# Serving a fifth of the tokens by fetched rows instead of dense expert tables, in a two-layer decoder step

## The chip, the cores and the metric

The kernel runs on one core of a Trainium2 chip. The metric is the device time of one execution in microseconds. TensorE multiplies matrices into the eight banks of PSUM, VectorE, ScalarE and GpSimd do the elementwise work between SBUF and PSUM, and DMA queues are fed by SyncE and GpSimd. Each engine runs its own instructions in order, and semaphores tie the engines together.

## What is computed

520 tokens (512 of a new sequence and 8 single ones) pass two layers. Layer 0 has a gated convolution beside attention, layer 1 a gated spatial mixer. After each comes an expert-retrieval mixer (PEER), which takes most of the time. For each token, and each of 8 heads, it picks 16 of 16,384 experts, an expert being one row of table U and one of table V, each 1024 floats:

```
q = (xf @ wq).reshape(n, PEER_HEADS, 2, PEER_DK // 2)
s = einsum('nhpd,hpkd->nhpk', q, keys);  top_s, top_i = top_k(s, 16)
best_s, pos = top_k(all 256 sums of a pair of top scores, 16);  gate = softmax(best_s)
hi = gelu(einsum('bed,bd->be', take(u_tab, ei), xi))      # 128 picks of each token
y  = einsum('be,bed->bd', gi * hi, take(v_tab, ei))
```

Then x becomes LayerNorm(alpha x + y). All is float32.

## The kernel before

Activations lie transposed: 8 blocks of 128 features in the partitions, 520 tokens in the columns. `xt` is x, `res` is alpha x, to which each mixer's result is added. A float32 product is made of three faster ones: ScalarE rounds a weight block to its high part (`whi`, `vhi`, `wth`), a subtraction gives the low part (`wlo`, `vlo`, `wtl`), and TensorE runs high x high, high x low and low x high.

The PEER mixer is dense: it computes every expert for every one of 512 tokens and masks with the gates. In each layer it has these stages.

**Queries.** `stage(C_WQ)` makes queries of 256 values per head for all 520 tokens, 16 chunks. GpSimd then loads the keys.

**First table.** 128 chunks (64 pairs, one slot of `whi`/`wlo`/`hid` each) of U, 128 experts a chunk: `chunk` runs 24 matmuls of 512 columns into `pstr[:, slot, 0]`, ScalarE takes gelu into `hid` (L753) and rounds the slot's next weights (L627), GpSimd makes the low part (L591), SyncE stores `hid` in HBM. Beside it runs the choice of experts, in five turns `w` of 104 tokens. TensorE computes the scores, VectorE ranks them (`topk`, some 160 short instructions in 48 parts, a Python generator), TensorE turns the picks, and ScalarE copies them to `pickt` (L800). In the next turn VectorE makes one-hot matrices of 4 tokens at a time (`one_hots`, L1311 once and L1314 four times), whose products on TensorE (L1553) are the dense gates; ScalarE copies them to `gst`, and SyncE stores them. `PLAN` gives the order: for each turn, how many pairs run with no gate group, with one behind each chunk, with two behind each chunk; ranking parts are dealt between one-hot groups by `RANK_PARTS` and `RANK_IN`.

**Second table.** 32 periods of 8 turns. A period covers 4 x 128 experts, a turn is 12 matmuls of 512 columns for one block of 128 output features (`second_table`, L1617). VectorE makes gated hidden values (`gated`, L1155 and L1157), their low part (L1162) and the low part of V (L1144), and adds each finished bank to `res` (`take_v`, L1170). ScalarE makes the two high parts (L821, L814). In a turn of even number the order on VectorE is gated, low part of V two turns ahead, add; on ScalarE it is high part of the gated values, then of V. The partial sums use two banks in turn.

The eight single tokens are not in the dense columns. GpSimd fetches their picked rows by indirect DMA (L604, 128 rows each, 8 times U and 8 times V a layer). VectorE multiplies and sums the rows of U (`sample_dot`, L1115) against x spread over all partitions by TensorE (L1637), and TensorE weights the rows of V (L1649).

Of the kernel before, what the change touches and what calls it, by code (L numbers as in the profile page):

```python
# [22 lines left out]
F32 = mybir.dt.float32  # L23
F32R = mybir.dt.float32r
# [29 lines left out]
WHOLE = SEQ // GH  # L54
# [13 lines left out]
assert all(2 * one + 4 * two == GROUPS for _, one, two in PLAN[1:])  # L68
# [16 lines left out]
DOTS_G, VALS_G = 1, 3  # L85
# [4 lines left out]
LN_OF = {2: 0, 3: 1, 5: 3}  # L90

# [32 lines left out]
def first_group(tt):  # L124

    return tt // NT * L_GROUPS + tt % NT * GROUPS

# [10 lines left out]
def trunk(nc, i, o):  # L138
    with ExitStack() as ctx:  # L139
# [17 lines left out]
        xl = place("xl", [P, KB, N], F32R)  # L157
        res = place("res", [P, KB, N], F32)
# [63 lines left out]
        s_id = place("s_id", [P, DEC], U32, choice_end + 2 * 4 * SEQ)  # L222
        s_idf = place("s_idf", [P, DEC], F32, choice_end + 2 * 4 * SEQ + 32)
        s_gate = place("s_gate", [P, DEC], F32, choice_end + 2 * 4 * SEQ + 64)

# [4 lines left out]
        wth = place("wth", [P, 2, GROUP, SEQ], F32R)  # L230
        wtl = place("wtl", [P, 2, GROUP, SEQ], F32R)
        gc = place("gc", [P, 2, 2 * NT, GROUP * GH], F32)
        hl = place("hl", [P, GROUP, SEQ], F32)
        wt = place("wt", [P, 2, SEQ], F32)


        rows = place("rows", [P, RING, D_MODEL], F32, at_xt)
        xr = place("xr", [DEC, 2, D_MODEL], F32R)
        pickr = place("pickr", [DEC, DEC], F32R)
        s_dots = place("s_dots", [P, DEC], F32)  # L240
        s_hid = place("s_hid", [P, DEC], F32)
        s_w = place("s_w", [P, DEC], F32)
        assert used[0] <= choice_end, used[0]

        hid = place("hid", [P, 2, SEQ], F32, choice_end)
        used[0] = choice_end + 2 * 4 * SEQ + 96
# [10 lines left out]
        gates = [nc.dram_tensor(f"gates{n}", (2 * NT, P, P, GH), F32, kind="Internal").ap() for n in range(DEPTH)]  # L257

        hidden = [nc.dram_tensor(f"hidden{n}", (P, P, SEQ), F32, kind="Internal").ap() for n in range(DEPTH)]
# [87 lines left out]

        s_listed = sem("s_listed")
        s_turned = sem("s_turned")
        s_rows = sem("s_rows")  # L350
        rows_in = [sem(f"rows_in{n}") for n in range(RING)]
        s_spread = sem("s_spread")
        s_dot = sem("s_dot")
# [1455 lines left out]
```

## Time and profile before

| | us |
|---|---|
| three runs | 4199.63, 4208.36, 4205.72; median 4205.72 |
| the profiled execution | 4195.6, its span 4193.8 |
| TensorE busy | 4040.5, 96% of the span |
| VectorE busy | 2710.7, 65% |
| ScalarE busy | 1478.5, 35% |
| GpSimd busy | 814.5, 19% |
| DMA | 648 MB, 155 GB/s on average |

Busy time is the union of an engine's instructions in the profiled execution. An engine that waits is not busy. TensorE's matmuls overlap, so the time one takes from start to end is longer than the distance from one start to the next, and it is the distance that adds up. The same holds by a smaller part for VectorE and ScalarE. Each layer's PEER mixer is some 1620 us: the first table from 572 and the second from 1452 us in layer 0, from 2555 and 3435 in layer 1.

### The profile page before, as it was taken

To read this page: it belongs to the slowest core of one execution; us is meant where nothing else is said; L and a number is where in the kernel's file an instruction comes from. 1 tells how busy PE (TensorE), PEld (TensorE's weight loads), DVE (VectorE), ACT (ScalarE), POOL (GpSimd) and SP (SyncE) were. 2 spreads that over 40 slices of the span, in tenths; PEclk is the share of its full clock that TensorE was granted. 3 is DMA by queue.
4 is the path that set the end of the run, shared out by engine and by line. 5 is a ranking of instruction groups with operands and counts; after the bars stand their busy time and mean duration, and the time that the engine had idled before them with its cause. 6 is when DMAs were issued, how large, how long until landed. Compare 5 with 4: busy or idle time off the path is not lost. (4 is left out here: it accounts for less than half of the span.)

```text
span 4193.8 us, 61594 instructions
## 1 busy us (share of the span) xinstructions
PE 4040.5 (96%) x20468; PEld 3334.9 (80%) x20468; DVE 2710.7 (65%) x5770; ACT 1478.5 (35%) x2092; POOL 814.5 (19%) x462
## 2 busy tenths in 40 slices
PE   8889899999999999999999899999999999999998
PEld 8734888888788788888879788888878878888887
DVE  2342367898887366777763336889889736677775
ACT  3221333444444322333334233444444432333333
POOL 4011123343333310000001012333333331000000
PEclk9989999999999999999999699999999999999999
DMA  4444233544454665655542023354444466555663
GB/s 121 126 141 137 77 111 121 172 154 150 148 172 146 237 216 171 201 193 195 189 138 71 25 76 115 117 177 153 146 165 152 167 215 219 189 191 186 199 198 106
DMA packets 315592, 648.24 MB, mean 155 GB/s; under 512 B 29496, under 2 KB 111544, under 8 KB 314832
## 3 DMA queue, kind: packets, MB, share of 16 engines
q1 hardware_dynamic: 302400, 606.66, 44.1%
q0 software_dynamic: 13072, 40.16, 3.2%
q8 instruction: 54, 0.88, 0.1%
q14 instruction: 66, 0.54, 0.0%
HBM read 507.09 MB, written 139.61 MB: 154 GB/s over the span
## 5 line engine op out<-in xcount | busy, mean ns | idle before, releaser
L591 POOL TENSOR_TENSOR wlo<-wraw,whi 128x1024 fp32r<-128x1024 f32 x252 | 646.9, 2568 | 1260.1 <-ACT whi L627 1260.1
L1356 PE MATMUL pstr<-xh,whi 128*128 128x512 f32 x2048 | 832.7, 407 | 12.0 <-POOL wlo L591 11.9
L1356 PE MATMUL pstr<-xh,wlo 128*128 128x512 f32 x2048 | 814.9, 398 | 0.0
L1617 PE MATMUL aux<-wth,vhi 128*128 128x512 f32 x2048 | 805.0, 393 | 7.1 <-DVE res L1170 7.1
L1356 PE MATMUL pstr<-xl,whi 128*128 128x512 f32 x2048 | 809.8, 395 | 0.0
L1617 PE MATMUL aux<-wth,vlo 128*128 128x512 f32 x2048 | 799.1, 390 | 0.0
L1617 PE MATMUL aux<-wtl,vhi 128*128 128x512 f32 x2048 | 798.7, 390 | 0.0
L1314 DVE TENSOR_SCALAR oh<-cst,pickt 128x128 f32<-128x128 f32 x1040 | 665.9, 700 | 0.0
L1144 DVE TENSOR_TENSOR vlo<-vraw,vhi 128x512 fp32r<-128x512 f32 x512 | 352.3, 688 | 325.7 <-ACT vhi L814 325.7
L821 ACT ACTIVATE wth<-wt 128x512 fp32r<-128x512 f32 x256 | 161.6, 632 | 933.7 <-DVE wt L1157 933.7
L753 ACT ACTIVATE hid<-pstr 128x512 f32<-128x512 f32 x256 | 152.8, 597 | 946.0 <-PE pstr L1356 931.8
L1356 PEld LDWEIGHTS pstr<-xh,whi 128*128 128x128 f32 x2048 | 388.7, 190 | 95.0 <-issue 15.1
L1356 PEld LDWEIGHTS pstr<-xh,wlo 128*128 128x128 f32 x2048 | 387.8, 189 | 92.1
L1617 PEld LDWEIGHTS aux<-wth,vhi 128*128 128x128 f32 x2048 | 385.6, 188 | 93.3 <-DVE vlo L1144 8.4
L1356 PEld LDWEIGHTS pstr<-xl,whi 128*128 128x128 f32 x2048 | 388.9, 190 | 84.6
L1617 PEld LDWEIGHTS aux<-wth,vlo 128*128 128x128 f32 x2048 | 385.3, 188 | 80.4
L1617 PEld LDWEIGHTS aux<-wtl,vhi 128*128 128x128 f32 x2048 | 385.7, 188 | 78.6
L1170 DVE TENSOR_TENSOR res<-res,aux 128x512 f32<-128x512 f32 x512 | 350.1, 684 | 135.1 <-PE aux L1617 133.3
L627 ACT ACTIVATE whi<-wraw 128x1024 fp32r<-128x1024 f32 x344 | 361.5, 1051 | 88.6 <-PE pstr L1360 85.9
L1311 DVE TENSOR_TENSOR oh<-cst,pickt 128x512 f32<-128x512 f32 x260 | 205.2, 789 | 227.5 <-PE aux L1553 169.5
L814 ACT ACTIVATE vhi<-vraw 128x512 fp32r<-128x512 f32 x512 | 298.7, 619 | 73.3 <-DMA vraw<-in_v 50.1
L889 DVE TENSOR_TENSOR wlo<-wraw,whi 128x1024 fp32r<-128x1024 f32 x92 | 113.3, 1233 | 325.4 <-ACT whi L627 325.4
(222 smaller groups left out, 4796.3 us busy)
## 6 DMA issues: line engine op xcount, KB each, us to landing
wraw<-in_u SPq DMA_DIRECT2D x256, 512.0 KB, 3.6
vraw<-in_v SPq DMA_DIRECT2D x512, 256.0 KB, 3.9
gates<-gst SPq DMA_DIRECT2D x80, 832.0 KB, 7.1
gc<-gates SPq DMA_DIRECT2D x64, 1040.0 KB, 5.5
hidden<-hid SPq DMA_DIRECT2D x256, 256.0 KB, 2.1
hl<-hidden SPq DMA_DIRECT2D x256, 256.0 KB, 4.9
wraw<-in_w SPq DMA_DIRECT2D x88, 512.0 KB, 3.5
kv<-in_ck SPq DMA_DIRECT2D x32, 256.0 KB, 3.2
```

The costliest lines, as they stand in the source:

```text
L591: e.tensor_tensor(wlo[:, slot, :], wraw[:, slot, :], whi[:, slot, :].bitcast(F32), ALU.subtract).then_inc(u_lo, 1)
L627: e.activation(whi[:, slot, :], wraw[:, slot, :], ACT.Copy).then_inc(w_hi, 1)
L753: e.activation(hid[:, slot, :], pstr[:, slot, 0, :], ACT.Gelu_apprx_tanh).then_inc(chunk_taken, 1)
L814: e.activation(vhi[:, v % 4, :], vraw[:, v % 4, :], ACT.Copy).then_inc(v_hi, 1)
L821: e.activation(wth[:, par, j, :], wt[:, j % 2, :], ACT.Copy).then_inc(wt_hi, 1)
L889: e.tensor_tensor(wlo[:, slot, :], wraw[:, slot, :], whi[:, slot, :].bitcast(F32), ALU.subtract).then_inc(w_lo, 1)
L1144: e.tensor_tensor(vlo[:, v % 4, :], vraw[:, v % 4, :], vhi[:, v % 4, :].bitcast(F32), ALU.subtract).then_inc(v_lo, 1)
L1170: e.tensor_tensor(r, r, aux[:, v % 2, :], ALU.add).then_inc(v_taken, 1)
L1311: e.tensor_tensor(oh2[:, slot], spread(c(IOTA), 1, shape), spread(pickt[:, 1, at:at + SUB], 2, shape), ALU.is_equal).then_inc(oh_ready, 1)
L1314: e.tensor_scalar(oh1[:, slot, r, :], c(IOTA), pickt[:, 0, at + r:at + r + 1], pickt[:, 2, at + r:at + r + 1], ALU.is_equal, ALU.mult).the ...
L1356: mm = e.matmul(pstr[:, slot, 0, :], w[:, slot, k * P:(k + 1) * P], x[:, k, 0:SEQ], start=k == 0 and w is whi and x is xh, stop=k == KB - ...
L1617: mm = e.matmul(aux[:, v % 2, :], w[:, v % 4, j * P:(j + 1) * P], x[:, par, j, :], start=j == 0 and w is vhi and x is wth, stop=j == GROUP ...
```

## The change

Of the 520 tokens the last 104 (`SPARSE`: one turn of the choice, which has the 8 single tokens and 96 others in it) leave the dense tables. `D` = 416 tokens stay, so every matmul, gelu, store and load of both tables has 416 columns. `hidden` and `gates` shrink accordingly, and gate groups fall from 130 to 104 a layer. The sparse tokens are ranked in the second turn (`ORDER`). Tokens lie in the partitions for them: one gather brings the row that pick j chose, for 104 tokens. A dot on VectorE against x (turned by TensorE in the query stage into two banks, `aux[:, 0:2]`) gives column j of `s_dots`. In the second table an add on VectorE sums 128 weighted rows of V into `acc`, which TensorE turns back at the end. GpSimd's loop is unrolled, with the gathers of U placed behind the low parts of given pairs.

The rows of U use the room of `res`, which is stored in HBM before (`keep`) and loaded again near the end. The second table's eight output blocks each stay in a bank of PSUM of their own over all 32 periods, so that `take_v` runs only in the last one. The one-hots read iota from a copy in PSUM. Scores go one round behind each of the first four chunks of a turn rather than all ahead of them.

```
+ND = 4
+D = ND * TT
+SPARSE = ND
+ORDER = [0, SPARSE, 1, 2, 3]
+NH = D // GH
-PLAN = [(6, 0, 0), (0, 11, 1), (0, 11, 1), (0, 9, 2), (0, 9, 2), (0, 1, 6)]
+PLAN = [(7, 0, 0), (2, 1, 6), (10, 0, 0), (2, 9, 2), (2, 9, 2), (0, 1, 6)]
-L_GROUPS = N // SUB
-EXP_AT = 17
+L_GROUPS = D // SUB
+EXP_AT = 20
-RANK_IN = 22
+RANK_FROM, RANK_TO = 1, 22
+DOTS = [0, 0, 22, 30, 30, 30]
+TAIL_DOTS = [10, 6]
+ADD_FROM, ADD_TO = 12, 236
...
+def share(n, total, begin, end):
+    return total * min(max(n - begin, 0), end - begin) // (end - begin)
+
+def row_pairs():
+    at, start = [], 0
+    for (zero, one, two), dots in zip(PLAN, DOTS):
+        for n in range(GROUPS):
+            if one + two:
+                pair = zero + (n // 2 if n < 2 * one else one + (n - 2 * one) // 4)
+                new = share(n + 1, dots, 0, GROUPS) - share(n, dots, 0, GROUPS)
+            else:
+                pair = 2 + n * (zero - 2) / GROUPS
+                new = share(n + 1, dots, 3, GROUPS) - share(n, dots, 3, GROUPS)
+            at += [start + pair] * new
+        start += zero + one + two
+    n = sum(TAIL_DOTS)
+    at += [start + TAIL * (k + 0.5) / n for k in range(n)]
+    return [int(at[max(j - RING, 0)]) + 1 for j in range(HJ)]
...
+        rows_u = place("rows_u", [P, RING, D_MODEL], F32, at_res)
+        rows_v = place("rows_v", [P, RING, D_MODEL], F32, at_xt)
...
+        v_banks = [aux[:, 2, :], aux[:, 3, :], pstr[:, 0, 1, :], pstr[:, 1, 1, :],
+                   pstr[:, 0, 0, :], pstr[:, 1, 0, :], aux[:, 0, :], aux[:, 1, :]]
+        iota = aux[:, 3, 0:P]
...
+                e.wait_ge(res_ready, 8 * (2, 4)[layer])
+                e.dma_start(keep[layer], res[:].rearrange("p k n -> p (k n)")).then_inc(res_out, 16)
                 load_u(0)
...
+                e.wait_ge(s_dot, (layer + 1) * HJ)
+                e.dma_start(res[:].rearrange("p k n -> p (k n)"), keep[layer]).then_inc(res_in, 16)
                 period(NG - 3, 1, True)
...
# GpSimd
+                def fetch_u(j):
+                    if j == 0:
+                        e.wait_ge(s_listed, layer + 1)
+                        e.wait_ge(res_out, 16 * (layer + 1))
+                    if j >= RING:
+                        e.wait_ge(s_dot, layer * HJ + j - RING + 1)
+                    e.indirect_dma_start(rows_u[0:TT, j % RING, :], None, i["ur"],
+                                         bass.IndirectOffsetOnAxis(ap=s_id[0:TT, j:j + 1], axis=0)).then_inc(rows_u_in[j % RING], 16)
-                with e.Fori(1, P // 2) as p:
+                fetch_at = row_pairs()
+                for p in range(1, P // 2):
                     for slot in range(2):
                         pair = p + C_U[layer] // 2
                         e.wait_ge(w_hi, pair * 2 + (slot + 1))
                         e.tensor_tensor(wlo[:, slot, :], wraw[:, slot, :], whi[:, slot, :].bitcast(F32),
                                         ALU.subtract).then_inc(u_lo, 1)
+                    for j in range(HJ):
+                        if fetch_at[j] == p or (fetch_at[j] > p and p == P // 2 - 1):
+                            fetch_u(j)
+                e.wait_ge(pick_ready, (layer + 1) * NT)
+                for j in range(HJ):
+                    if j >= RING:
+                        e.wait_ge(s_acc, layer * HJ + j - RING + 1)
+                    e.indirect_dma_start(rows_v[0:TT, j % RING, :], None, i["vr"],
+                                         bass.IndirectOffsetOnAxis(ap=s_id[0:TT, j:j + 1], axis=0)).then_inc(rows_v_in[j % RING], 16)
...
# VectorE
+                def sparse_dots(n):
+                    for _ in range(n):
+                        j = next(dots)
+                        if j == 0:
+                            e.wait_ge(s_turned, layer + 1)
+                            e.wait_ge(s_listed, layer + 1)
+                        e.wait_ge(rows_u_in[j % RING], 16 * (layer * (HJ // RING) + j // RING + 1))
+                        row = rows_u[0:TT, j % RING, :]
+                        e.scalar_tensor_tensor(row, row, 1.0, aux[0:TT, 0:2, :].rearrange("p a n -> p (a n)"), ALU.mult, ALU.mult,
+                                               accum_out=s_dots[0:TT, j:j + 1]).then_inc(s_dot, 1)
+                def sparse_add(j):
+                    e.wait_ge(rows_v_in[j % RING], 16 * (layer * (HJ // RING) + j // RING + 1))
+                    row, weight = rows_v[0:TT, j % RING, :], s_w[0:TT, j:j + 1]
...
+                        e.wait_ge(s_acc, layer * HJ + j)
+                        e.scalar_tensor_tensor(acc[0:TT], row, weight, acc[0:TT], ALU.mult, ALU.add).then_inc(s_acc, 1)
...
+                        for n in range(GROUPS):
+                            one_hots(layer * L_GROUPS + d * GROUPS + n, n % 2, n * SUB)
+                            for _ in range(share(n, RANK_PARTS, RANK_FROM, RANK_TO), share(n + 1, RANK_PARTS, RANK_FROM, RANK_TO)):
+                                next(ranking, None)
+                            sparse_dots(share(n + 1, DOTS[w], 0, GROUPS) - share(n, DOTS[w], 0, GROUPS))
...
+                for g in range(NG):
+                    par, more = g % 2, g + 1 < NG
+                    if not more:
+                        e.wait_ge(res_in, 16 * (layer + 1))
+                    for v in range(8):
+                        if more and v % 2 == 0:
+                            gated(g + 1, v // 2, 1 - par, (g + 1) // 2)
+                        elif more:
+                            split_wt(g + 1, v // 2, 1 - par)
+                        if v < 6:
+                            split_v(g, v + 2)
+                        elif more:
+                            split_v(g + 1, v - 6)
+                        if (g, v) == (1, 2):
+                            sparse_weights()
+                        while added < share(g * 8 + v + 1, HJ, ADD_FROM, ADD_TO):
+                            sparse_add(added)
+                            added += 1
+                        if not more:
+                            take_v(v)
+                        if not more and v in (4, 5):
+                            take_back(v - 4)
...
# one_hots
-                e.tensor_tensor(oh2[:, slot], spread(c(IOTA), 1, shape), spread(pickt[:, 1, at:at + SUB], 2, shape),
+                e.tensor_tensor(oh2[:, slot], spread(iota, 1, shape), spread(pickt[:, 1, at:at + SUB], 2, shape),
                                 ALU.is_equal).then_inc(oh_ready, 1)
                 for r in range(SUB):
-                    e.tensor_scalar(oh1[:, slot, r, :], c(IOTA), pickt[:, 0, at + r:at + r + 1],
+                    e.tensor_scalar(oh1[:, slot, r, :], iota, pickt[:, 0, at + r:at + r + 1],
                                     pickt[:, 2, at + r:at + r + 1], ALU.is_equal, ALU.mult).then_inc(oh_ready, 1)
...
# TensorE
+                def turn_x():
+                    e.wait_ge(ln_out, 8 * LN_OF[split] + 8)
+                    for k in range(KB):
+                        mm = e.transpose(aux[0:TT, k // 4, k % 4 * P:(k % 4 + 1) * P], xt[:, k, D:N], c(IDENT))
+                    mm.then_inc(s_turned, 1)
+                stage(C_WQ[layer], N_WQ, split, between=turn_x)
...
+                            mm = e.matmul(v_banks[v][:, 0:D], w[:, v % 4, j * P:(j + 1) * P], x[:, par, j, :],
+                                          start=isinstance(g, int) and g == 0 and j == 0 and w is vhi and x is wth,
+                                          stop=isinstance(g, int) and g == NG - 1 and j == GROUP - 1 and w is vlo)
```

## Rows read from the trace of the kernel before

**Rows 1.** Busy time of each engine by stage, granted clock, DMA share and GB/s last.

```profile
572.00:1452.00 880.00, 859.56 (x4286) 718.37 (x4285) 695.44 (x1708) 373.01 (x431) 328.37 (x130) 0.99 0.47 158
1452.00:2189.00 737.00, 733.05 (x3281) 604.18 (x3280) 499.07 (x902) 221.10 (x385) 14.43 (x14) 1.00 0.58 188
2555.00:3435.00 880.00, 859.70 (x4286) 718.60 (x4285) 695.29 (x1708) 372.99 (x431) 327.49 (x130) 0.99 0.47 158
...
1620.00:2100.00 480.00, 480.00 (x2119) 397.63 (x2119) 339.09 (x618) 151.54 (x264) 0.00 (x0) 1.00 0.60 193
```

**Rows 2.** Timeline: two chunks apart on ScalarE; matmuls of 260 columns. Start, duration.

```profile
1397.36 0.60 ACT L753 ACTIVATE hid<-pstr 128x512 f32<-128x512 f32 x1 [3.71 <-PE pstr L1356]
...
1408.52 0.60 ACT L753 ACTIVATE hid<-pstr 128x512 f32<-128x512 f32 x1 [4.12 <-PE pstr L1356]
...
540.10 0.40 PE L1360 MATMUL pstr<-xh,wlo 128*128 128x260 f32 x2
540.34 0.41 PE L1360 MATMUL pstr<-xh,whi 128*128 128x260 f32 x2
```

**Rows 3.** Timeline of TensorE, first matmuls of two chunks with a gate group between.

```profile
2720.87 0.48 PE L1356 MATMUL pstr<-xh,whi 128*128 128x512 f32 x1
...
2727.34 0.48 PE L1356 MATMUL pstr<-xh,whi 128*128 128x512 f32 x1
```

**Rows 4.** Timeline of VectorE, a ranking's first and last instructions.

```profile
576.11 3.19 DVE L1216 MAX8 tv<-scores 104x8 f32<-104x128 f32 x16 [2.39 <-ACT scores L780]
...
632.01 0.29 DVE L1301 TENSOR_TENSOR pick<-bv,gs 104x128 f32<-104x128 f32 x1
```

**Rows 5.** Groups of VectorE by shape: busy, mean ns of one, idle before.

```profile
L1115 DVE SCALAR_TENSOR_TENSOR rows<-rows,pstr 128x1024 f32<-128x1024 f32 x16 | 19.5, 1220 | 0.7
...
L1000 DVE SCALAR_TENSOR_TENSOR t<-zp,vec,t 128x512 f32<-128x512 f32 x8 | 6.0, 752 | 0.3
```

**Rows 6.** VectorE: one-hots in the timeline; MAX8's min/median/max; the one-hots' group.

```profile
3275.49 0.68 DVE L1311 TENSOR_TENSOR oh<-cst,pickt 128x512 f32<-128x512 f32 x1
...
3277.11 0.68 DVE L1311 TENSOR_TENSOR oh<-cst,pickt 128x512 f32<-128x512 f32 x1
...
3280.27 3.21 DVE L1314 TENSOR_SCALAR oh<-cst,pickt 128x128 f32<-128x128 f32 x4
...
L1216 DVE MAX8 tv<-scores x160: 264/275/296, 576.1 to 3129.2; 104x8 f32<-104x128 f32 x160
...
L1314 DVE TENSOR_SCALAR oh<-cst,pickt 128x128 f32<-128x128 f32 x1040 | 665.9, 700 | 0.0
```

**Rows 7.** Timeline of GpSimd, one split late in the first table.

```profile
1404.48 2.41 POOL L591 TENSOR_TENSOR wlo<-wraw,whi 128x1024 fp32r<-128x1024 f32 x1 [3.10 <-ACT whi L627]
```

**Rows 8.** The gathers: issue on GpSimd in ns, min/median/max; time to landing.

```profile
L604 POOL DMA_INDIRECT rows<-in_ur,s_id x16: 937/1146/1251, 1442.1 to 3489.7; - x16
...
DMA to landing us min/median/max: 4.1/4.9/7.7
```

**Rows 9.** The chain that ended last: start, us, one spread and one value round.

```profile
3466.63 1.12 PE pstr L1637 x4
...
3526.48 1.68 PE aux L1649 x16
```

**Rows 10.** Timelines of VectorE and ScalarE in the second table; then waits: us, times, longest.

```profile
3702.38 0.64 DVE L1155 TENSOR_TENSOR wt<-hl,gc 128x468 f32<-128x468 f32 x1
3702.93 0.20 DVE L1157 TENSOR_TENSOR wt<-hl,gc 128x44 f32<-128x44 f32 x1
3704.34 0.69 DVE L1144 TENSOR_TENSOR vlo<-vraw,vhi 128x512 fp32r<-128x512 f32 x1 [1.22 <-ACT vhi L814]
3704.95 0.68 DVE L1170 TENSOR_TENSOR res<-res,aux 128x512 f32<-128x512 f32 x1
...
3703.16 0.63 ACT L821 ACTIVATE wth<-wt 128x512 fp32r<-128x512 f32 x1 [3.77 <-DVE wt L1157]
...
ACT vhi L814 <- DMA vraw<-in_v: 50.1, 84, 1.4
```

More of the change, by code:

```diff
@@ L776, in peer @@
                     tt = w + layer * NT
-                    if w < NT:
+                    first = pair
+                    if w == 0:
                         for b in range(4):
-                            e.wait_ge(sc_done, tt * 4 + b + 1)
-                            e.activation(scores[0:TT, 4 * b:4 * b + 4, :].rearrange("p a k -> p (a k)"),
-                                         aux[0:TT, 2 + b % 2, :], ACT.Copy).then_inc(sc_taken, 1)
-                    if zero:
-                        hidden_pair(pair)
-                        with e.Fori(pair + 1, pair + zero - 2) as p:
+                            take_scores(tt, b)
+                    elif w < NT:
+                        for r in range(4):
+                            hidden_one(first + r // 2, r % 2)
+                            take_scores(tt, r)
+                        first += 2
+                    if zero and not one + two:
+                        if first == 0:
+                            hidden_pair(first)
+                            first += 1
+                        with e.Fori(first, pair + zero - 1) as p:
                             hidden_pair(p)
                         gate_exponentials(tt)
-                        for p in range(pair + zero - 2, pair + zero):
-                            hidden_pair(p)
+                        hidden_pair(pair + zero - 1)
                     n = 0
@@ L1363, in chunk, with stage @@
                 mm.then_inc(chunk_done, 1)
-            def stage(first, count, split, means=None):
+            def stage(first, count, split, means=None, between=None):
                 chunk(first, 0, 0, split)
                 chunk(first, 0, 1)
+                if between:
+                    between()
                 start = count // 2 - 3
@@ L1559, in first_table, with score_round @@
                         chunk(C_U[layer], pair, slot)
+                def score_round(w, b):
+                    tt, d = w + layer * NT, ORDER[w]
+                    if w and b == 0 and ORDER[w - 1] != SPARSE:
+                        e.wait_ge(pick_taken, layer * ND + ORDER[w - 1] + 1)
+                    if tt or b:
+                        e.wait_ge(sc_taken, tt * 4 + b)
+                    for q in range(4 * b, 4 * b + 4):
+                        mm = e.matmul(aux[0:TT, 2, q % 4 * P:(q % 4 + 1) * P], q_t[:, q, d * TT:(d + 1) * TT], keys[:, q, :],
+                                      start=True, stop=True)
+                    mm.then_inc(sc_done, 1)
                 pair = 0
@@ L1563, in peer @@
                     tt = w + layer * NT
[L1564 removed]
+                    first = pair
+                    if w == 0:
                         for b in range(4):
[L1567 to L1577 removed]
+                            score_round(w, b)
+                        first_table(0)
+                        first += 1
+                    elif w < NT:
+                        for r in range(4):
+                            chunk(C_U[layer], first + r // 2, r % 2)
+                            score_round(w, r)
+                        first += 2
+                    if first < pair + zero:
+                        with e.Fori(first, pair + zero) as p:
                             first_table(p)
[L1579 to L1581 removed]
+                    pair += zero
+                    if one + two:
+                        n = layer * L_GROUPS + ORDER[w - 1] * GROUPS
                         def one_group_each(q):
@@ L1652, in period, with mean_after @@
+                def mean_after(blocks):
+                    for k in blocks:
+                        e.wait_ge(v_taken, layer * KB + max(k + 1, 2))
+                        e.wait_ge(s_added, layer * 2 + k // 4 + 1)
+                        mm = mean_block(res, k, aux[:, 2:4])
+                    return mm
                 def period(g, par):
```

337 lines of the change are left out of this document (131 added, 206 removed).

## The prediction, before the result was known

> **What bounds the kernel now.** I read the busy time by stage first. Each layer's feed-forward part is two stages: the first table (scores, ranking, one-hots, gates beside 64 pairs of chunks), 572 to 1452 us, and the second table, 1452 to 2189. The reader is to see TensorE busy for 860 of 880 us and 733 of 737, VectorE for 695 and 499, at granted clock 0.99 and 1.00, the 2.4 GHz level [rows 1]. Layer 1 repeats the first stage within 0.4 us of busy time on every engine, so every saving counts twice. TensorE bounds both, so I then looked in the timeline for what one matmul costs by its columns, and last for the slack of the engines beside it, because the change moves work from TensorE onto VectorE.
>
> **TensorE, first table.** Two chunks, 48 matmuls of 512 columns, take 1408.52-1397.36 = 11.16 us, 0.2325 each; 260-column matmuls start in pairs 0.24 apart, 0.120 each [rows 2]. The difference, 0.1125 for 252 columns, is 0.43 ns a column up to rounding of the pair: the time follows the columns, down to 260, so no floor of the weight load stands above 416. At 2.4 GHz 96 columns are 0.040 us. 3072 matmuls save 123 us a layer; a chunk falls from 5.58 to 4.62. A gate group costs 2727.34-2720.87 = 6.47 less a chunk of 5.58, 0.89 us [rows 3]; 130 become 104: 23 us. TensorE alone would need 880-123-23 = 734 us.
>
> **VectorE, first table.** It has: 5 rankings of 632.3-576.1 = 56.2 us [rows 4]; 104 one-hot groups (were 130); 128 new dots. A dot has the form of L1115, now with 104 partitions: 1.22, and the accumulator read lies behind it, so 1.15 from start to start by the overlap of neighbours [rows 5]; I take 1.15. A one-hot group has two prices today: 3277.11-3275.49 = 1.62 when GpSimd is idle, and about 2.1 more when four L1314 take 3.21 beside a GpSimd split [rows 6]. The change feeds these from a copy of iota in PSUM. A one-input instruction like MAX8 never exceeded 296 ns in 160 tries, with splits every 5.6 us [rows 6], so an instruction which takes one operand from SBUF isn't held. I take 1.62; bounds 1.4 (no row of one-column-per-cycle work goes under MAX8's) and 3.2 (the mean of before: 665.9/1040 = 0.64 a L1314, four of them, and 0.60 for L1311).
> The Trainium skill, "SBUF — State Buffer", section "Who interferes with whom", says the same of the cause: the port pair shared with GpSimd is locked for a whole instruction by VectorE's double-rate mode or two SBUF inputs, and not by an instruction with at most one SBUF input at single rate. By that rule the group costs 1.62 or slightly more; without it, rival B.
>
> Sum: 281+168+147 = 596 us of 734. That fits, but not in each window, since ranking starts only when the scores are out, which now go one round behind each of the first four chunks: 4 x 4.62 + 4 x 0.9 = 22.2 us in. Window by window, TensorE against VectorE:
> (2,1,6): 18 chunks 83.2 + scores 3.7 + 26 groups 23.1 + turn 1 = 111; 22.2+56.2+24 x 1.62 = 117. Over by 6.
> (10,0,0): 92.4+3.7+1 = 97; 22.2+56.2+22 x 1.15+1.6 for handing on = 105. Over by 8.
> (2,9,2), twice: 120.1+3.7+23.1+1 = 148; 22.2+56.2+38.9+28 x 1.15 = 149.5. Over by 2, with the last groups 3 each.
> The first window (7 pairs, 64.7, and scores, against 56.2 plus scores), the last and the tail are TensorE's. Together 20. The new gathers sit in GpSimd's queue behind both splits of a pair, and each waits for the dot four before it; behind it waits the next split, and for that TensorE. A split is 2.4 us and, in the tail of the stage, GpSimd waits 3.10 between splits [rows 7]; chunks that are 0.96 shorter leave 2.2. Two gathers of 1.15 [rows 8] fit and a third is 1.2 late, of which TensorE feels 0.5 to 0.8, only where VectorE is the bound already. Rows can also come late for their dot: nothing to 6 us (issue and landing, 1.15+4.9 [rows 8]) in each of three windows; I take 3, 9 in all. Stage: 734+20+9 = 763, down 117.
>
> **Second table.** TensorE: the window 1620 to 2100 has 2119 matmuls in 480 us, 0.2265 [rows 1]; less 0.040 is 0.1865, and 3072 of them save 123. The samples' own work goes: 8 spreads of 1.12 and 8 value rounds of 1.68 [rows 9], 22 us; turning their x goes too, and turning the sparse sum back comes, alike. TensorE alone: 737-123-22 = 592.
> VectorE loses 512 additions into res (sums stay in the eight banks) and gains 128 adds of 1024 columns a layer in 224 of 256 turns, 1.14 per two turns. Its old cost falls, but not its wait. Per two turns it issues gated; then waits while ScalarE rounds wth and then vhi, from 3703.13 to 3704.34, 1.21 us; then splits, subtracts, splits [rows 10]. That wait was hidden beside TensorE and is filled by nothing in the new order. Columns cost (0.64-0.20)/(468-44) = 1.04 ns there, so gated is 0.59 and a 416-column split 0.50; a 512-column one stays 0.61 apart. An add has the form of L1000 (two SBUF inputs, 752 ns at 512 [rows 5]); 512 more columns make 1.29, overlapping by 0.08: 1.21. Bounds for it: 1.15 (the dot) and 1.50 (twice L1000). Sum: 0.59 + (1.21-0.08, since 96 of 512 columns of the 0.63 of wth are 0.12 at most) + 0.61+0.50+0.60 + 1.14 x 1.21 = 4.81, against 24 x 0.1865 = 4.48 for TensorE. So VectorE's chain with ScalarE is late next: 28 periods of 4 x 4.81 = 19.2 instead of 17.9 add 37. Stage: 592+37 = 629, down 108. The add's rows are hidden: four buffers and an add every 4.2 us leave 16.8 us for 1.15+4.9. The bound for the gathers in sum: v, h, gates and rows are 2.10+0.85+0.85+1.95 = 5.75 MB a period; at 193 GB/s for a DMA share of 0.60 [rows 1], a full share is 322 and 5.75 MB take 17.9 us, under 19.2 but not by much.
>
> **Elsewhere.** Turning the 104 tokens' x in the query stage: 16 passes, twice a gate group's 8 [rows 3], about 2 us a layer. Keeping res (2.1 MB) lies beside that stage's last chunks; its return is waited for only in the last period, some 35 us after its issue, and takes 7 us of the DMA engines at 322 GB/s: nothing, or up to 7 if v is late behind it. +4 in all.
>
> **Sum.** 4195.6 - 2 x (117+108) + 4 = 3749.6. The profiled execution stands 10 below the median of 4205.7; added, 3760.
>
> **Rivals.**
> A. TensorE bounds all. VectorE's leads smooth the windows and the chain. For it: 596 of 734 us, and only 0.33 per two turns over. Against: the wait of 1.21 is in the order of the instructions. 734 and 592: 4195.6-2x(146+145)+4+10 = 3628.
> B. One-hots stay held by the splits. For it: today's 3.21. Against: MAX8. 1.5 us more in each of 104 groups where VectorE is the bound, 156 a layer: 3760+312 = 4072.
> C. The DMA engines are too full: v lands late, and ScalarE's wait adds onto the chain. For it: 5.75 MB would be a share of 0.93; ScalarE waits for v up to 1.4 already [rows 10]. Against: a load is asked for four turns, 9 us, ahead. Half of 1.4 in each two turns is 0.7 x 112 = 78 a layer: 3916.
> D. Slower. Gathers are served one after another, four buffers or not: issue 1.15, landing 4.9, use 1.2 = 7.3 us, x 128 = 934 us in each stage: 3760+2x(171+305) = 4712. In the first table the splits queue behind them. Decides from about 6.3 us a gather ((763+112)/128 and (629+112)/128, averaged). For it: before's gathers each waited for a buffer, so none shows two in flight under pressure. Against: landing is 4.1 to 7.7 with other loads running, and only the 1.15 is on GpSimd.
> The Trainium skill, "SBUF — State Buffer", section "SBUF: two separate sides", tells of gather descriptors that can't be written while VectorE runs at double rate; in the second table VectorE has none of these, and the issue stayed at 1.15 beside its two-input work, so the rule adds little to D.
>
> **How the numbers follow.** Forecast 53 in 100, with its own range 3680 to 3850 (add 1.15 to 1.50, windows 0 to twice their excess). A 17, C 17, B 8, D 5. The range 3610 to 3930 holds the forecast, A and the lower part of C and leaves out B, D and the rest. Faster by over 0.2% (what a measurement here tells from no change) 94, within 1, slower 5.
>
> **What would show it.** Matmuls 0.192 and 0.187 apart; no L1314 near 2.5 us; stages near 763 and 629; in the second TensorE waits for vlo or wtl, VectorE still for vhi at 1.1, and a period is 19.2 (17.9: A; over 21: C). ScalarE's wait for v over 50 us would show C, gathers landing 6.3 us apart with VectorE waiting for rows D. I am wrong if a stage exceeds before's, or one-hots keep their 3.21.

## The result, and the profile after

The changed kernel takes 4331.07 us (median of 4 runs, 4323.10 to 4335.91) against 4203.68 for the kernel before (median of 4): 1.030 times as long, interval 1.0289 to 1.0318. The forecast was 3760. Slower, and outside the range.

Four stretches tell where. From the first matmul of the scores to the first of the second table is the first table, from there to the last the second table. The first two rows are layer 0, the third is the piece of the second table that stood in [rows 1], the last the first table of layer 1; columns as there.

```profile
575.00:1511.20 936.20, 747.24 (x4076) 725.99 (x4077) 631.38 (x1826) 337.30 (x404) 444.12 (x255) 0.89 0.61 190
1511.20:2256.40 745.20, 629.16 (x3098) 587.75 (x3097) 451.19 (x646) 214.22 (x382) 191.85 (x128) 0.96 0.89 237
1620.00:2100.00 480.00, 402.66 (x1975) 371.86 (x1973) 300.73 (x421) 136.24 (x244) 143.42 (x94) 0.97 0.92 244
2626.60:3562.20 935.60, 749.93 (x4077) 729.18 (x4078) 632.02 (x1826) 337.28 (x404) 446.54 (x255) 0.89 0.61 190
```

Each of the two stages should have lost over 100 us, and each gained: 936 where 763 was forecast (before 880), 745 where 629 was (before 734). 173 and 116 too much, in both layers: 579 us, which is the whole miss of 571 but for a few us. TensorE did lose its work (747 of 936 us against 860 of 880), but no engine took its place. In the first table TensorE and VectorE both idle for a fifth or more of the stage. In the second the DMA share is 0.92 where it was 0.60, for only 244 GB/s against 193.

The waits of the kernel after say for what (engine, line, tile, releaser: us in all, times, longest):

```profile
POOL wlo L641 <- ACT whi L675: 942.3, 213, 93.0
DVE vlo L1213 <- ACT vhi L873: 537.9, 288, 7.2
DVE rows_u L1171 <- DMA rows_u<-in_ur,s_id: 328.1, 65, 21.6
ACT vhi L873 <- DMA vraw<-in_v: 274.0, 157, 5.9
PE pstr L1633 <- DVE oh L1384: 190.2, 64, 10.3
POOL rows_u L633 <- DVE rows_u L1171: 146.2, 54, 9.0
PE pstr L1426 <- POOL wlo L641: 93.0, 16, 20.4
```

Two waits stand out: the dots (L1171), which are new, wait for fetched rows, and ScalarE's wait for v has grown from 50.1 [rows 10] to 274.0. The others pass these on: the gate products (L1633) wait for one-hots that stand behind a dot, the chunks (L1426) for splits that stand behind a gather (L633).

**The first table.** The chain of waits through the last choice window (start, us, what) shows the whole loop:

```profile
1332.17 2.42 POOL wlo L641
1334.59 0.17 issue
1334.76 6.14 DMA rows_u<-in_ur,s_id
1340.92 1.23 DVE rows_u L1171 x2
1342.15 0.60 DVE oh L1381
1342.76 1.28 DVE oh L1384 x4
1344.03 1.13 DVE rows_u L1171 x2
1345.17 0.60 DVE oh L1381
1345.77 1.29 DVE oh L1384 x4
1347.06 0.12 issue
1347.18 2.07 PE pstr L1633 x8
1349.25 5.41 PE pstr L1426 x24
1354.70 0.39 issue
1355.10 1.06 ACT whi L675
1356.22 2.40 POOL wlo L641
```

It closes on itself: split, gather, landing, dot, one-hots, gate products, chunk, rounding, next split. One turn of it is 1356.22-1332.17 = 24.05 us, for one pair of chunks, where TensorE needs 2 x 4.62 + 4 x 0.89 = 12.8. The timeline of GpSimd in the same pair:

```profile
1334.76 0.97 POOL L633 DMA_INDIRECT rows_u<-in_ur,s_id  x1 [0.17 <-issue]
...
1338.59 0.97 POOL L633 DMA_INDIRECT rows_u<-in_ur,s_id  x1 [0.30 <-issue]
1342.45 0.98 POOL L633 DMA_INDIRECT rows_u<-in_ur,s_id  x1 [2.90 <-DVE rows_u L1171]
1343.44 2.40 POOL L641 TENSOR_TENSOR wlo<-wraw,whi 128x1024 fp32r<-128x1024 f32 x1
```

Five gathers stand behind one pair's splits. Four are issued at once, since the four buffers are free; the fifth waits for a dot of a row that was only just asked for, and the next split waits behind it. So buffers run empty and are filled in bursts: in this window the dots wait for a landing in pair after pair (11.70 us before the one at 1340.92).

**The second table.** One piece of its chain of waits:

```profile
1696.12 7.11 DMA vraw<-in_v
1703.34 0.64 ACT vhi L873
```

Here the load of a block of v, 0.26 MB, lands after 7.1 us (median of all 6.9, before 3.9); over the whole stage such landings are 34% of the chain. VectorE's timeline between such arrivals is the one forecast:

```profile
1776.01 0.58 DVE L1223 TENSOR_TENSOR wt<-hl,gc 128x416 f32<-128x416 f32 x1
1777.73 0.69 DVE L1213 TENSOR_TENSOR vlo<-vraw,vhi 128x512 fp32r<-128x512 f32 x1 [1.14 <-ACT vhi L873]
1778.34 1.28 DVE L1187 SCALAR_TENSOR_TENSOR acc<-rows_v,s_w,acc 104x1024 f32<-104x1024 f32 x1
1779.54 0.58 DVE L1228 TENSOR_TENSOR wtl<-wt,wth 128x416 fp32r<-128x416 f32 x1
...
1780.64 0.59 DVE L1223 TENSOR_TENSOR wt<-hl,gc 128x416 f32<-128x416 f32 x1
```

1780.64-1776.01 = 4.63 us for two turns, the wait for ScalarE 1.14 (forecast 1.13), an add 1.20 from start to start (forecast 1.21). What such turns don't explain of the stage is put down to late loads; the experiments below test it.

The queues of the page (packets, MB, share of 16 engines), first of before, then of after:

```profile
q1 hardware_dynamic: 302400, 606.66, 44.1%
q0 software_dynamic: 13072, 40.16, 3.2%
```

```profile
q1 hardware_dynamic: 284288, 562.75, 42.2%
q0 software_dynamic: 82192, 241.56, 21.7%
```

A queue's MB over its share of the span is what it would move at a full share: q1 606.66/(0.441 x 4193.8) = 328 GB/s before and 308 after, q0, which has the gathers, 299 and 257. In before only 16.8 of q0's 40.16 MB are gathers, after 218 of 241.56. The bytes of the new gathers take more of the engines than others'.

### The profile page after: what moved, and what is told of

Same layout as the page of the kernel before. It is cut to its first block, busy times and chain, and to the rows that moved or that the text cites. A ratio compares the mean times of both kernels' runs of the same rounds, so it can differ in the third digit from the quotient of the medians.

```text
span 4334.2 us, 58245 instructions
## 1 busy us (share of the span) xinstructions
PE 3623.5 (84%) x19726; PEld 3328.2 (77%) x19726; DVE 2493.2 (58%) x5496; ACT 1392.6 (32%) x2034; POOL 1406.8 (32%) x942
## 3 DMA queue, kind: packets, MB, share of 16 engines
q0 software_dynamic: 82192, 241.56, 21.7%
## 4 chain that ended last, share of the span: by engine, by line
PE 43%; DVE 23%; DMA 18%; issue 6%; ACT 5%; POOL 2%; SPq 2%; ACTq 0%; DVEq 0%; POOLq 0%
PE pstr L1426 18%; DMA vraw<-in_v 12%; PE pstr L1430 12%; DMA rows_u<-in_ur,s_id 5%; DVE acc L1187 4%; DVE vlo L1213 3%; DVE oh L1384 3%; ACT vhi L873 2%; DVE rows_u L1171 2%; PE pstr L1633 2%; PE pstr L1716 2%; POOL wlo L641 2%; PE aux L1716 2%; DVE wt L1223 2%; PE pstr L1558 1%
## 5 line engine op out<-in xcount | busy, mean ns | idle before, releaser
L1426 PE MATMUL pstr<-xh,whi 128*128 128x416 f32 x2048 | 763.8, 373 | 93.6 <-POOL wlo L641 93.0
L1426 PE MATMUL pstr<-xl,whi 128*128 128x416 f32 x2048 | 742.4, 363 | 0.0
L1426 PE MATMUL pstr<-xh,wlo 128*128 128x416 f32 x2048 | 740.8, 362 | 0.0
L652 POOL DMA_INDIRECT rows_v<-in_vr,s_id x256 | 385.3, 1505 | 971.3 <-DVE acc L1187 884.2
L1716 PE MATMUL pstr<-wth,vhi 128*128 128x416 f32 x1024 | 390.5, 381 | 161.5 <-DVE vlo L1213 161.5
L1171 DVE SCALAR_TENSOR_TENSOR rows_u<-rows_u,aux 104x1024 f32<-104x1024 f32 x256 | 309.4, 1214 | 329.7 <-DMA rows_u<-in_ur,s_id 328.1
L1426 PEld LDWEIGHTS pstr<-xh,whi 128*128 128x128 f32 x2048 | 406.4, 198 | 105.0 <-issue 89.2
L1716 PE MATMUL aux<-wth,vhi 128*128 128x416 f32 x1024 | 370.6, 362 | 69.2 <-DVE wtl L1228 55.0
L1633 PE MATMUL pstr<-oh,oh 128*128 128x128 f32 x1664 | 251.3, 302 | 190.4 <-DVE oh L1384 190.2
L873 ACT ACTIVATE vhi<-vraw 128x512 fp32r<-128x512 f32 x512 | 306.4, 622 | 317.8 <-DMA vraw<-in_v 274.0
L1426 PEld LDWEIGHTS pstr<-xl,whi 128*128 128x128 f32 x2048 | 404.5, 198 | 4.8
L1426 PEld LDWEIGHTS pstr<-xh,wlo 128*128 128x128 f32 x2048 | 402.3, 196 | 5.2
L1633 PEld LDWEIGHTS pstr<-oh,oh 128*128 128x128 f32 x1664 | 234.5, 211 | 207.5 <-issue 119.2
L1716 PE MATMUL pstr<-wtl,vhi 128*128 128x416 f32 x1024 | 376.3, 368 | 0.0
L1716 PE MATMUL pstr<-wth,vlo 128*128 128x416 f32 x1024 | 375.6, 367 | 0.0
L1716 PE MATMUL aux<-wth,vlo 128*128 128x416 f32 x1024 | 360.9, 352 | 0.0
```

The lines of the kernel that those rows point to most:

```text
L652: e.indirect_dma_start(rows_v[0:TT, j % RING, :], None, i["vr"], bass.IndirectOffsetOnAxis(ap=s_id[0:TT, j:j + 1], axis=0)).then_inc(rows_ ...
L873: e.activation(vhi[:, v % 4, :], vraw[:, v % 4, :], ACT.Copy).then_inc(v_hi, 1)
L1171: e.scalar_tensor_tensor(row, row, 1.0, aux[0:TT, 0:2, :].rearrange("p a n -> p (a n)"), ALU.mult, ALU.mult, accum_out=s_dots[0:TT, j:j + ...
L1426: mm = e.matmul(pstr[:, slot, 0, 0:D], w[:, slot, k * P:(k + 1) * P], x[:, k, 0:D], start=k == 0 and w is whi and x is xh, stop=k == KB - ...
L1633: mm = e.matmul(pstr[:, slot, 1, r * P:(r + 1) * P], oh2[:, slot, r, :], oh1[:, slot, r, :], start=True, stop=True)
L1716: mm = e.matmul(v_banks[v][:, 0:D], w[:, v % 4, j * P:(j + 1) * P], x[:, par, j, :], start=isinstance(g, int) and g == 0 and j == 0 and w ...
```

## The experiments

Theory 1, first table: the loop above, from placing gathers behind the splits that TensorE waits for, in bursts larger than the ring. Theory 2, second table: the DMA engines are full, and part of it is that a gather of 104 rows is dear for its bytes. Rivals: VectorE has too much to do in both (its 128 dots and adds); or one-hots held, as before. Stage times are of layer 0; layer 1 agrees within 10 us. e1 to e4, e8 and e9 were run once, the others two to eight times; the runs of one kernel lay within 0.35%.

| kernel | first table | second table | us |
|---|---|---|---|
| before | 880.5 | 733.6 | 4203.7 |
| after | 936.2 | 745.2 | 4331.1 |
| e1 rows of 256 columns | 887.8 | 649.6 | 4055.9 |
| e2 sums of 256 columns | 901.5 | 719.2 | 4211.4 |
| e3 no gathers | 775.0 | 636.7 | 3793.3 |
| e4 96 rows | 911.7 | 687.4 | 4177.7 |
| e5 112 rows | 922.7 | 698.9 | 4207.6 |
| e6 gathers behind single chunks | 856.7 | 741.5 | 4163.4 |
| e7 e5+e6, dots dealt evenly | 824.8 | 693.6 | 4009.7 |
| e8 e3, iota from SBUF | 824.0 | 637.1 | 3888.7 |
| e9 e3, sums of 4 columns | 751.3 | 589.0 | 3654.0 |
| e10 e7, gathers a chunk earlier | 823.2 | 692.6 | 3998.3 |

**e1: a quarter of each row.** The gathers bring 256 of 1024 columns; dots and adds keep their size, on stale data. The sparse sum is left out of `res` in e1 to e4, e8 and e9, and e1, e3, e8 and e9 clear the row buffers once a layer and have one more wait on GpSimd behind the first table's splits.

```
-rows_u[0:TT, j % RING, :], None, i["ur"],
+rows_u[0:TT, j % RING, 0:256], None, i["ur"].rearrange("n (a c) -> (n a) c", a=4),
... (the same for V)
```

> Every gather brings 256 of 1024 columns (a quarter of the bytes, same number, same places in GpSimd's order); dots and adds stay 1024 wide; the sparse sum is left out of res. Stages of the changed kernel in layer 0: first table 936 us, second 745 us. Theory 'full DMA': the second table is set by the bytes of the gathers beside v, h and gates; it should fall to what I had for VectorE's chain, 625 to 650. Rival 'VectorE': the adds set it; it stays within 15 us of 745. First table, theory 'loop' (a gather waits in GpSimd's queue behind the splits, the splits for chunks, the chunks for gate groups, these for dots, these for the gather): landing falls from 7.7 to about 5 us, so each turn of the loop loses some 3 us and the stage falls only to 880 to 910. Rival 'bytes' there too: it falls under 800.

The landing of a V row falls from 8.3 us (median) to 4.5, and the second table to 650, near the 629 of the chain: it was the bytes. The first table stays at 888, though U rows land in 3.8 instead of 7.7: shorter landings shorten the loop, and don't remove it.

**e2: a quarter of each sum.** Full rows are fetched, dots and adds work on 256 columns.

```
-row = rows_u[0:TT, j % RING, :]
+row = rows_u[0:TT, j % RING, 0:256]
...
-e.scalar_tensor_tensor(acc[0:TT], row, weight, acc[0:TT], ALU.mult, ALU.add)
+e.scalar_tensor_tensor(acc[0:TT, 0:256], row, weight, acc[0:TT, 0:256], ALU.mult, ALU.add)
```

> Gathers are whole; dots and adds read 256 of the 1024 columns, so VectorE loses about 0.8 us of each; the sparse sum is left out of res. 'Full DMA': the second table stays at 725 to 745, though VectorE has 100 us less to do. 'VectorE': it falls to about 600. First table, 'loop': each turn of the loop has one to three dots in it and the landing stays, so 880 to 920. 'VectorE' there: under 830.

Both stages end just about where 'full DMA' and 'loop' have them (719 where 725 was the lowest; 901.5). A piece of its second table, columns as above:

```profile
1600.00:1850.00 250.00, 215.78 (x1055) 206.47 (x1056) 123.93 (x229) 75.61 (x135) 71.21 (x51) 0.94 0.98 255
```

VectorE is busy for 124 of 250 us, and the stage still takes 719. The DMA engines are at 0.98 and move 255 GB/s, and v lands so late that ScalarE waits 423.2 us for it. With 104-row gathers in the mix 255/0.98 = 260 GB/s is all there is. To relieve VectorE gave 35 us in the first table and 26 in the second, of 173 and 116 too much: it isn't the main cause in either, and the rival falls as the main cause.

**e3: no gathers.** Dots and adds are all done, on what the buffers hold.

```
-e.indirect_dma_start(rows_u[0:TT, j % RING, :], ...)
-e.indirect_dma_start(rows_v[0:TT, j % RING, :], ...)
```

> No gathers at all, dots and adds run at full width on cleared buffers at once; the sparse sum is left out of res. 'Loop': the first table falls to 763 to 790, what my sum had for it without late rows. If instead the first table's loss came from the one-hots or the order of scores, it stays above 860. Second table: VectorE's chain with ScalarE alone, 625 to 640; TensorE alone would be 592.

Its two stages:

```profile
572.90:1347.90 775.00, 716.96 (x4077) 702.43 (x4078) 634.47 (x1829) 334.49 (x404) 316.01 (x126) 0.96 0.46 160
1347.90:1984.60 636.70, 600.06 (x3097) 572.69 (x3096) 449.05 (x644) 210.38 (x382) 0.00 (x0) 1.00 0.58 191
```

775 and 637 against the forecast's 763 and 629, which held nearly nothing for gathers. So all but 20 us a layer of the miss is the gathers': 161 in the first table, 108 in the second. Its waits, which are the ones to compare others with (both layers):

```profile
PE pstr L1630 <- DVE oh L1381: 80.1, 34, 6.5
ACT vhi L865 <- DMA vraw<-in_v: 50.3, 79, 1.2
PE pstr L1423 <- POOL wlo L640: 17.2, 9, 5.0
```

**e4 and e5: 96 and 112 rows.** Is it the bytes alone? e4 fetches 8% fewer than 104 (its dots and adds have 96 partitions too), e5 8% more (8 rows of dummy index, dots and adds as they were).

```
-rows_u[0:TT, ...   s_id[0:TT, j:j + 1]
+rows_u[0:96, ...   s_id[0:96, j:j + 1]      # e4
+rows_u[0:112, ...  s_id[0:112, j:j + 1]     # e5
```

> Gathers, dots and adds on 96 partitions instead of 104; 8 tokens' experts are left out, and the sparse sum is left out of res. Theory 'spread': 104 rows are dealt unevenly to the 16 DMA engines and 96 evenly, so landing falls by a fifth or more (7.7 and 8.3 us to under 6.5) and both stages by over 30 us. Rival 'bytes': 8% fewer bytes, landing down by under 0.7 us, the second table by 10 to 25 us, the first by under 15.

> Only the gathers change: 112 rows instead of 104 (8 padding rows of index 0; dots and adds as they were), 8% more bytes. 'Spread' (96 rows took 57 us off the second table and landing from 8.3 to 5.8 us, more than 8% of the bytes can): 112 is a multiple of 16 as 96 is, so landing is near 6.5 us and the second table 695 to 720 instead of 745; the first table 915 to 935. 'Bytes': landing and the stage grow, 755 or more.

e4: landings of 6.2 us (U) and 5.8 (V), and 58 us less in the second table, where 'bytes' allowed 25. The first table loses 24.5, short of the 30 that 'spread' had for it. More bytes, less time: e5 takes 0.9715 of the change's time (4207.61 over 4331.07) and is 1.0017 times before (1.0006 to 1.0029), and its second table is 46 us shorter than with 104 rows. The queues of e5:

```profile
q1 hardware_dynamic: 284288, 562.75, 40.9%
q0 software_dynamic: 74000, 258.29, 20.1%
```

258.29/(0.201 x 4207.5) = 305 GB/s at a full share, against 257 with 104 rows; the landing of a V row is 6.2 us instead of 8.3, and ScalarE's wait for v 166.4 instead of 274.0. The Trainium skill, "DMA: Bandwidth & Descriptors", section "Why a DMA increments its semaphore by 16 and not by 1", has a rule that fits the landings: a transfer is spread over the largest number of engines, up to 16, that divides its rows. By it 104 rows go over 13 engines, 8 each, and 96 and 112 over 16, 6 or 7 each. The landings agree in their order; no view shows the engines of one gather.

The number of engines doesn't by itself explain the 257, since a share counts only time in packets. The traces have each packet's time: one of a gather's 4 KB packets (the queue's, less e3's) takes 254 ns in the mean with 104 rows (251 in e2, 254 in e6), but 221 with 96 and 212 with 112 (217 in e7; 212 with before's 128). There are also more packets: the page's count less that of e3 (8464), over 512 gathers, is 144 for 104 rows and 128 for 112, 40 and 16 more than the rows; the added ones have 4 bytes and little time. So it is shown that 104 rows are dear; why a packet is slower then stays open.

**e6: gathers behind single chunks.** A gather of U is placed behind a single split, by the chunk (not the pair) at which the dot four before it is due, and two chunks later.

```
-for j in range(HJ):                       # behind both splits of a pair
-    if fetch_at[j] == p or ...: fetch_u(j)
+        for j in range(HJ):               # behind the split of each slot
+            if fetch_at[j] == 2 * p + slot: fetch_u(j)
-return [int(at[max(j - RING, 0)]) + 1 for j in range(HJ)]
+return [min(int(at[max(j - RING, 0)]) + 2, P - 1) for j in range(HJ)]
```

> Only the places of U's gathers in GpSimd's queue change: behind the split of a slot, two chunks after the dot that frees the buffer, instead of in bundles behind a pair's second split. 'Loop': rows come about one chunk earlier and one by one; the first table falls from 936 to 830 to 880; the second stays at 745. Rival: the engines' order is not the cause but the landing time under load; the first table stays over 915.

Nothing but the order in GpSimd's queue is changed, and the first table falls by 79.5 us, half of the gathers' cost; the second stays at 742. The wait of the dots for rows falls from 328.1 to 167.3. Ratio to before 0.9911 (0.9892 to 0.9931).

**e7: both repairs, and an even deal.** e5 and e6, and the dots dealt so that no window has more than 2.6 a pair (before up to 4.3):

```
-DOTS = [0, 0, 22, 30, 30, 30]
+DOTS = [0, 0, 26, 34, 34, 18]
```

> Both at once, and the dots dealt by the number of pairs in a turn: 26, 34, 34, 18 instead of 22, 30, 30, 30. 'Loop': the crowded turn (30 dots in 7 pairs) is relieved: first table 800 to 850; with 112 rows the second is 695 to 720. The time is 4194-2x(60+28) = about 4020, faster than both kernels.

4009.67 us, ratio 0.9545 (0.9524 to 0.9565): faster than both. Its waits, as above:

```profile
ACT vhi L873 <- DMA vraw<-in_v: 162.4, 118, 3.8
DVE rows_u L1172 <- DMA rows_u<-in_ur,s_id: 103.9, 41, 13.2
PE pstr L1634 <- DVE oh L1385: 94.0, 37, 7.3
PE pstr L1427 <- POOL wlo L641: 75.0, 23, 14.5
```

The first table is 825, 50 above e3. The even deal wasn't run alone; of the 32 us between e6 and e7 in the first table, the 112 rows gave 13 in e5.

The first table by turns of the choice, from the starts of the 128 activations that write `hid` (layer 0, us):

| pairs | after | e3 | e6 | e7 |
|---|---|---|---|---|
| 7 | 71 | 71 | 71 | 71 |
| 9, `(2, 1, 6)` | 134 | 134 | 134 | 131 |
| 10 | 117 | 100 | 118 | 114 |
| 13 | 185 | 167 | 179 | 183 |
| 13 | 184 | 160 | 164 | 165 |
| 7, `(0, 1, 6)` | 163 | 88 | 109 | 87 |
| the last 5 | 82 | 55 | 81 | 74 |

The last choice window, whose loop is shown above, holds 76 of the 161. e6 takes 54 of these away and e7 the other 22, with 18 dots there instead of 30 and 112 rows a gather. The rest lies in smaller parts in the turns before it and in the last 5 pairs, and e7 keeps most of that.

**e8: iota from SBUF.** e3 with the one-hots reading iota where the kernel before did.

```
-e.tensor_tensor(oh2[:, slot], spread(iota, 1, shape), ...
+e.tensor_tensor(oh2[:, slot], spread(c(IOTA), 1, shape), ...
-e.tensor_scalar(oh1[:, slot, r, :], iota, ...
+e.tensor_scalar(oh1[:, slot, r, :], c(IOTA), ...
```

> As the kernel with no gathers (first table 775, second 637), but the one-hots read iota from SBUF again; the sparse sum is left out of res. If GpSimd's splits hold them as before, L1314's like take 3.2 us for four beside a split against 1.28 from PSUM: over 104 groups up to 1.5 us each, of which part is behind TensorE: first table 810 to 900. If iota's place does nothing: 770 to 780, or a little less, since four from SBUF alone took 1.02.

The first table grows from 775 to 824. The one-hots' tile, in e8 and then in after (ns, min/median/max):

```profile
L1381 DVE TENSOR_SCALAR oh<-cst,pickt x832: 327/336/2579, 646.6 to 3170.1; 128x128 f32<-128x128 f32 x167
```

```profile
L1384 DVE TENSOR_SCALAR oh<-aux,pickt x832: 392/402/413, 648.8 to 3479.1; 128x128 f32<-128x128 f32 x167
```

From SBUF the instruction is faster when free (336) and held up to 2579; from PSUM it takes 402 and never over 413 (452 in e3). The copy is worth 49 us a layer, in a kernel without gathers.

**e9: the floor.** e3 with dots and adds on 4 columns.

```
-row = rows_u[0:TT, j % RING, :]
+row = rows_u[0:TT, j % RING, 0:4]
... (the adds likewise)
```

> As e3 (no gathers, the sparse sum left out of res), and the 128 dots and 128 adds work on 4 columns instead of 1024, so that VectorE is nearly relieved of the sparse part. Theory (the prediction's sum): TensorE alone sets 734 and 592 us; what is left above it is the ranking and one-hots in the window (2,1,6), 22.2+56.2+24x1.87 = 123 against 111, so a first table of about 746 and a second of 592 to 600, and 3793 - 2x(29+40) = 3655 us. Rival (TensorE has a floor of its own above the columns' cost, or ScalarE's chain holds the second table without the adds): second table stays above 615.

```profile
575.50:1326.80 751.30, 711.33 (x4077) 698.30 (x4078) 504.31 (x1832) 334.16 (x404) 309.75 (x126) 0.98 0.48 165
1326.80:1915.80 589.00, 585.94 (x3096) 579.57 (x3095) 316.49 (x640) 211.59 (x382) 0.00 (x0) 1.00 0.64 206
```

751.3 and 589.0 against 746 and 592 to 600, and 3654.0 us against 3655. TensorE's part of the sum holds, and the sums on VectorE cost 24 us in the first table and 48 in the second, as e3 has both.

**e10: one chunk earlier.**

```
-return [min(int(at[max(j - RING, 0)]) + 2, P - 1) for j in range(HJ)]
+return [min(int(at[max(j - RING, 0)]) + 1, P - 1) for j in range(HJ)]
```

> e7 with each gather of U placed one chunk earlier in GpSimd's order (one chunk instead of two behind the estimated place of the dot it waits for). Theory (loop through GpSimd's queue): the gather's wait for its dot now comes ahead of a split more often and holds the chunk, so the first table is longer than e7's 825 and 832 by 5 to 40 us; second table as e7's. Rival (rows land late, an earlier issue helps whatever stands behind it): the first table is shorter than e7's by 10 us or more.

Neither: 823.2 and 821.8 in the two layers against e7's 824.8 and 831.8. GpSimd waits more for dots (191.3 against 88.2 us) and the dots less for rows (78.0 against 103.9), and the two nearly cancel. 3998.27 us, ratio 0.9511 (0.9495 to 0.9527): the best version run, its interval just meeting e7's. Once gathers go singly and the dots are dealt evenly, a chunk sooner or later matters little. That speaks for the burst as what mattered in e6, which had changed both the burst and the place; no run has the one without the other.

## Why the prediction was wrong

**The steps that held.** TensorE alone, 734 and 592: e9 gives 751 (its forecast, 746, had one window over) and 589, and the second table's matmuls stand 0.189 apart (48 in 9.07 us of the chain). The first held as a sum, not window by window: `(2, 1, 6)` takes 134 in after and e3 alike, where 117 was forecast; that wasn't taken apart. A dot 1.15: 1342.07-1340.92 in the timeline. The second table's chain, 629: e3 gives 637, e1 650, and the wait of 1.13 is there at 1.14. Idle time before a ranking, 22.2, was somewhat high: VectorE waits ten times for the scores, 176.2 us in all, 17.6 each. Elsewhere, +4: what lies outside the four stages grew from 966.1 to 971.6.

**The one-hot group**, 1.62, was too small: its two rows in the chain make 0.60 + 1.28 = 1.88. A read from PSUM isn't held (413 ns at most in after and 452 in e3, against 2579 in e8), so rival B is false, but it has a price of its own, 0.40 instead of 0.34. In the prediction's own sum that is 24 x 0.26 = 6 us in each of the three windows where VectorE and its one-hots were the bound. The sum without late rows was 734+20 = 754, and e3 has 775; an estimate of 18 of these 21 us is thus the one-hots'. The Trainium skill, "SBUF — State Buffer", section "Who interferes with whom", names as the cause that two SBUF inputs or the double rate lock the port pair shared with GpSimd and an instruction with at most one SBUF input at single rate doesn't. e8 beside e3 agrees with it.

**The first failed step: "Rows can also come late for their dot: nothing to 6 us ... in each of three windows; I take 3, 9 in all", and beside it "a third is 1.2 late".** Measured: 936 - 775 = 161 a layer. The text had the order in GpSimd's queue right and priced it by the time to issue alone. It asked if three gathers fit in the 2.2 us between splits, and separately, once a window, if rows come late. But a gather behind a split also waits for a dot, and so for a landing, and the dot waits in front of the one-hots that lead to the split: each pair pays the landing and the chunk in turn, not beside each other. In the last window the deal of 30 dots over 7 pairs (4.3 a pair, four buffers) makes this certain; the two rows 24.05 apart show it, against 12.8. e6 shows it by the order alone: 79.5 of the 161. With the 112 rows and the even deal 111 are gone (e7), and 50 remain. They are not the waits for one-hots, which e3 has nearly as long (94.0 against 80.1 in both layers); more has grown of TensorE's waits for GpSimd's splits (75.0 against 17.2), that is 29 a layer. The rest was not taken apart.

**The second: "a full share is 322 and 5.75 MB take 17.9 us, under 19.2 but not by much".** The text put the loads at nothing because their mean rate sufficed. Two things were wrong in that.

First, late loads cost time before the rate is reached. In e7 it is not reached:

```profile
1600.00:1850.00 250.00, 223.01 (x1120) 206.59 (x1119) 169.94 (x238) 77.50 (x141) 82.27 (x54) 0.99 0.87 270
```

270/0.87 = 310 GB/s at a full share, close to the 322, and a period's 5.90 MB (rows of 112) take 19.0 us, still under 19.2. Yet the stage is 57 us above e3's. The time is in ScalarE's wait for v. Stage (layer 0) and wait (half of both layers') above e3's, in us, for the runs with adds at full width:

| | second table | wait for v |
|---|---|---|
| e1 | 13 | 15 |
| e4 | 51 | 59 |
| e5 | 62 | 58 |
| e6 | 105 | 114 |
| e7 | 57 | 56 |
| after | 108 | 112 |

So the wait for v, which the text had at nothing, accounts for the whole 108, within 10 us in every run.

Second, 322 was worked out from a mix with next to no gathers. With 104-row gathers in it, a full share is 244/0.92 = 265 GB/s (260 in e2): 5.75 MB take 21.7 us, over the chain's 19.2, which by the rate alone makes 592 + 28 x (21.7 - 17.9) = 698. The shape of the gather is worth 46 us of the stage (e5), and no row of before could show it, since its gathers had 128 rows.

So rival C had the mechanism, and its sign came (ScalarE's wait for v over 50 us: 274.0). Its price, 629 + 78 = 707, is near e5 and e7 (699, 694), in part by luck: it took half of before's longest wait in each two turns, 78 a layer, where e7 has 56 more than e3.

**Rival D** as stated is false: a V row lands after 8.3 us (median) and is then used for 1.2, which times 128 would be over 1200 us in a stage of 745, so gathers do overlap. The issue on GpSimd, taken to stay at 1.15, had a mean of 1.51 in the second table. Its side remark, that the splits queue behind the gathers, was the real one. It had 5 in 100 because its price was tied to service one by one. **Rival A** asked for no chain; e3's 637 against e9's 589 shows there is one.

The chance for slower, 5 in 100, was too low since the two costs that I had bounded apart, late rows in three windows and loads, were each bounded as if the ring were steady and the engines as free as before.

## What to carry to other kernels

When a new DMA is put in an engine's queue, follow the loop: what waits behind it, what that feeds, and whether the wait in front of it is at the end of the same loop. If so, each turn pays the landing in full; issue singly, where its buffer has long been free, and never more between two links than the ring holds. When forecasting a fuller DMA, take the full-share rate from a row with the same kind and shape of transfer, or let the range reach down by a fifth, and price late loads even where the mean rate suffices: at a share of 0.87 they cost 57 us of 694 here. Try rounding the rows of a gather up to a multiple of 16: 112 rows cost less than 104.

## What the runs showed of the hardware

- The queue of the gathers moved 257 GB/s at a full share with 104 rows a gather and 305 with 112. Less what the same queue moves in e3 (23.38 MB in 2.1% of 3791.3 us), the gathers alone come to 253, 307 and, with 96 rows, 294; for before's 128 rows rounding leaves 286 to 332.
- Issuing a gather took GpSimd 1.15 us in before. In after the median is 0.98 in the first table and 1.07 in the second, but the mean is 1.08 and 1.51, and single ones take up to 3.04 and 2.17. In the second table it fell to a mean of 1.35 when the adds had a quarter of the columns (e2) and to 1.11 with 96 rows (e4), and stayed at 1.48 with 112 (e5); what holds it was not isolated.
- A wait on TensorE cost more than its own length. From 1300 to 1400 us it was busy for 63 us, and the granted clock was 0.79, a mean between the two levels (2.4 GHz is 1.00, 1.2 GHz 0.50); the chunks behind long waits took 5.41 to 5.51 us, not 4.62. Over the whole first table the clock was 0.89, in e3 0.96. In e7, where it was busy for 97 of the 100 us from 1250 to 1350, the clock was 1.00:

```profile
1300.00:1400.00 100.00, 63.47 (x332) 60.84 (x331) 51.26 (x116) 32.36 (x35) 39.54 (x28) 0.79 0.67 201
```

```profile
1250.00:1350.00 100.00, 96.71 (x591) 95.61 (x590) 70.49 (x161) 51.40 (x58) 60.77 (x40) 1.00 0.88 309
```
